# Search passes dealt to attention heads by summed engine loads in place of weights

## What is computed

```
dots  = relu(einsum('bqhd,bsd->bqhs', q_idx, k_idx))
score = einsum('bqh,bqhs->bqs', w_idx, dots)          # -inf where not visible
_, idx = top_k(score, 256)                            # ties to the lower index
out_b = softmax(q . k[idx] * 64**-0.5 - slope * |t - idx|) @ v[idx]
```

## Time and profile before

| | us |
|---|---|
| median of 3 runs (3246.18 to 3248.87) | 3247.67 |
| profiled execution | 3250.48 |
| its span | 3248.7 |
| TensorE busy (share of the span) | 2896.0 (89%) |
| VectorE busy | 1690.7 (52%) |
| ScalarE busy | 1570.1 (48%) |
| GpSimd busy | 320.7 (10%) |

### The profile page before, as it was taken

The page is one execution under the profiler, slowest core; times in us unless marked ns, Lnnn a source line. Parts: engine busy times, 40 slices in busy tenths (PEclk is TensorE's granted clock), DMA queues, the critical chain, the costliest instruction groups (busy, mean ns, idle before and its releaser), DMA issues. The chain is left out here.

```text
span 3248.7 us, 42237 instructions
## 1 busy us (share of the span) xinstructions
PE 2896.0 (89%) x14392; PEld 2341.5 (72%) x14392; DVE 1690.7 (52%) x3092; ACT 1570.1 (48%) x3006; POOL 320.7 (10%) x1001
## 2 busy tenths in 40 slices
PE   6578888787977897889898999999999999999998
PEld 3456566666766676678786888878888888888887
DVE  2246768686978868845454444244432544244433
ACT  0457787778787786884433222232223222232222
POOL 0112231212121120110011000000000000000000
PEclk8788988899988988899999999999999999999999
DMA  5000000000000001121456333343333433343333
GB/s 211 7 23 14 24 14 14 14 14 14 14 4 14 10 7 56 59 108 42 127 177 192 97 97 97 123 143 97 97 118 112 133 97 97 120 145 97 93 99 119
DMA packets 286884, 254.86 MB, mean 78 GB/s; under 512 B 8685, under 2 KB 238617, under 8 KB 286617
## 3 DMA queue, kind: packets, MB, share of 16 engines
q1 hardware_dynamic: 282584, 236.32, 23.4%
q10 hardware_dynamic: 4160, 16.78, 1.3%
HBM read 219.50 MB, written 33.57 MB: 78 GB/s over the span
## 5 line engine op out<-in xcount | busy, mean ns | idle before, releaser
L2045 ACT ACTIVATE p_hi<-raw 128x1024 fp32r<-128x1024 f32 x264 | 279.4, 1058 | 669.5 <-PE ubank L1979 339.1
L2124 DVE TENSOR_TENSOR p_lo<-raw,p_hi 128x1024 fp32r<-128x1024 f32 x264 | 323.4, 1225 | 405.1 <-ACT p_hi L2045 405.1
L1322 DVE TENSOR_SCALAR_CACHE_REDUCE above<-score,cand 128x384 uint8<-128x384 f32 (+6 forms) x224 | 315.8, 1410 | 4.4
L1172 ACT ACTIVATE signs<-score,pick 128x512 int8<-128x512 f32 (+6 forms) x224 | 304.4, 1359 | 27.7 <-POOL pick L684 19.2
L1150 ACT ACTIVATE logit<-tbank 128x512 f32<-128x512 f32 (+3 forms) x448 | 214.3, 487 | 210.7 <-PE tbank L903 207.8
L903 PE MATMUL tbank<-ident,logit 128*128 128x128 f32 x1336 | 252.4, 303 | 63.5 <-ACT logit L1140 56.0
L919 PE MATMUL obank<-vb,logit 128*128 128x64 f32 x2176 | 299.8, 283 | 0.0
L919 PEld LDWEIGHTS obank<-vb,logit 128*128 128x128 f32 x2176 | 293.7, 208 | 0.0
L1977 PE MATMUL gbank<-x_hi,p_hi 128*128 128x512 f32 x704 | 276.5, 393 | 14.8 <-DVE p_lo L2124 14.8
L788 PE MATMUL work<-w_in,h_T 128*128 128x512 f32 (+1 forms) x768 | 282.7, 515 | 0.7 <-ACT h_T L981 0.7
L1978 PE MATMUL gbank<-keys,p_hi 128*128 128x512 f32 x704 | 275.9, 392 | 0.0
(11 more groups left out here) (236 smaller groups left out, 5133.4 us busy)
## 6 DMA issues: line engine op xcount, KB each, us to landing
raw<-in_w_gate_up SPq DMA_DIRECT2D x176, 512.0 KB, 3.8
raw<-in_w_down SPq DMA_DIRECT2D x88, 512.0 KB, 3.8
w_in<-in_w_ada ACTq DMA_DIRECT2D x4, 4096.0 KB, 13.0
wada<-in_w_ada SPq DMA_DIRECT2D x4, 2048.0 KB, 15.6
row<-in_x SPq DMA_DIRECT2D x16, 512.0 KB, 3.9
mixT<-oT SPq DMA_DIRECT2D x32, 256.0 KB, 2.3
x_rows<-in_x SPq DMA_DIRECT2D x16, 512.0 KB, 4.6
x<-x_rows SPq DMA_DIRECT2D x16, 512.0 KB, 3.1
```

The costliest lines, as they stand in the source:

```text
L1172: nc.scalar.activation(signs[:, 0:L], score[:, b % 2, 0:L], ACT.Sign, scale=-1.0, bias=pick[:].bitcast(F32), accum_out=less_more[:]).then_ ...
L1322: link(nc.vector.tensor_scalar(above[:, 0:L], score[:, b % 2, 0:L], cand[:].bitcast(F32), None, ALU.is_ge, ALU.add, accum_out=count[:]), b ...
L2045: nc.scalar.activation(p_hi[:, s], raw[:, s], ACT.Copy).then_inc(panel_high, 1)
L2124: nc.vector.tensor_tensor(p_lo[:, s], raw[:, s], p_hi[:, s].bitcast(F32), ALU.subtract).then_inc(panel_ready, 1)
```

## The change

The weights and `spread` go. `loads` walks the list of steps without any search in it and adds up, for each slot, an estimate of what VectorE, ScalarE and TensorE do there, at rates written as constants; work that an engine does some heads later is put to the later slot. `deal_passes` first adds the closing steps. Then it goes 32 rounds; in each, every search places one pass in the slot of its window where the longest of the three sums grows least, with 0.15 of the engine's own sum and 0.1 for each pass already there added. A window begins at the slot behind which the scores are complete, as heads 0 to 3 of the A group. `all_steps` makes the list once with empty searches and once with the dealt ones; a step now carries its slot as well, so the two lists are its entries 5 and 6. The instructions themselves, the closing steps and every other step are as before.

```diff
...
-def vector_weight(b, slot):
...
-def scalar_weight(b, slot):
...
-def spread(weights, n):
...
 def search_slots(b):
...
         slots += [(it, "B", h) for h in range(HEADS)]
+    return slots
...
+COLUMN = 1.05
+FIXED = 0.06
+PASS_VECTOR = 0.39
+PASS_SCALAR = 0.50
+SIDE = {"vector": {"norm": 1.3, "gains": 0.9, "latent": 0.8, "latent_up": 1.2, "queries": 1.5},
+        "scalar": {"norm": 1.3, "transposes": 1.2, "latent": 2.8, "latent_up": 2.8, "queries": 3.0, "mod": 0.6},
+        "tensor": {"transposes": 1.0, "latent": 0.7, "latent_up": 2.2, "queries": 1.3, "mod": 4.0}}
+PROJ = {"vector": (0, 0, 0, 0, 0), "scalar": (0, 0.6, 0, 0.6, 2.2), "tensor": (3.5, 3.5, 3.5, 3.5, 2.8)}
+def streamed(cols):
+    return FIXED + COLUMN * cols / 1000
+def loads(steps, beside):
+    out = {"vector": {}, "scalar": {}, "tensor": {}}
+    slots, it = [], {}
+    for s in steps:
+        if s[0] == "head":
+            slots.append(s[4])
+    heads = [s[1:4] for s in steps if s[0] == "head"]
+    for engine in out:
+        out[engine] = {slot: 0.0 for slot in slots}
+    def put(engine, at, us):
+        if 0 <= at < len(slots):
+            out[engine][slots[at]] += us
+    i = -1
+    for s in steps:
+        if s[0] == "head":
+            i += 1
+            kind, b, h = s[1:4]
+            tiles = len(key_tiles(kind, b))
+            for _, n in key_chunks(kind, b):
+                put("vector", i, streamed(n) + 0.1)
+                put("tensor", i, 0.92 * n / 1000)
+                put("scalar", i + 2, streamed(n))
+            put("tensor", i + 2, 0.12 * tiles)
+            put("tensor", i + 3, 0.23 * tiles)
+            put("scalar", i + 1, streamed(P * tiles) + 0.35 + (0.3 if kind == "A" else 0))
+            if h == HEADS - 1:
+                put("vector", i + 4, 1.0)
+                put("tensor", i + 5, 0.5)
+                put("scalar", i + 6, 0.6)
+            continue
+        at = i if s in beside else i + 1
+        if s[0] == "scores":
+            n = key_chunks("B", s[1])[s[2]][1]
+            put("vector", at, IDX_HEADS * (streamed(n) + 0.1))
+            put("scalar", at, IDX_HEADS * streamed(n))
+            put("tensor", at, IDX_HEADS * 0.92 * n / 1000)
+            continue
+        for engine in out:
+            us = PROJ[engine][s[2]] if s[0] == "proj" else SIDE[engine].get(s[0], 0.0)
+            lag = LAG[engine].get(s[0], 0) if engine != "tensor" and s in beside else 0
+            put(engine, at + lag, us)
+    return out
+def deal_passes(load):
     vector, scalar = {}, {}
-    if searched_by_scalar(b):
-        wts = [scalar_weight(b, slot) for slot in slots[:-3]]
-        for slot, r in zip(slots, spread(wts, len(ON_SCALAR))):
-            scalar[slot] = [(b, ON_SCALAR[n]) for n in r]
-        for slot, action in zip(slots[-3:] + slots[-1:], AFTER_SCALAR):
+    searched = [b for b in range(NB) if P * (b + 1) > TOPK]
+    windows, counts = {}, {}
+    for b in searched:
+        slots = search_slots(b)
+        each = streamed(P * (b + 1))
+        scored = len(key_chunks("B", b))
+        if searched_by_scalar(b):
+            closing = zip(slots[-3:] + slots[-1:], AFTER_SCALAR)
+            windows[b] = slots[scored - 1:-3]
+        else:
+            closing = zip(slots[-2:] + slots[-1:], SEARCH[-3:])
+            windows[b] = slots[scored - 1:-2]
+        for slot, action in closing:
             vector.setdefault(slot, []).append((b, action))
-    else:
-        wts = [vector_weight(b, slot) for slot in slots[:-2]]
-        for slot, r in zip(slots, spread(wts, len(SEARCH) - 3)):
-            vector[slot] = [(b, SEARCH[n]) for n in r]
-        for slot, action in zip(slots[-2:] + slots[-1:], SEARCH[-3:]):
-            vector.setdefault(slot, []).append((b, action))
+            load["vector"][slot] += each * {"above": 1, "bias": 1}.get(action[0], 4 if action[1] == 0 else 2)
+        counts[b] = {slot: 0 for slot in windows[b]}
+    def longest(slot):
+        return max(load[engine][slot] for engine in load)
+    for _ in range(32):
+        for b in searched:
+            engine = "scalar" if searched_by_scalar(b) else "vector"
+            own = streamed(P * (b + 1)) + (PASS_SCALAR if engine == "scalar" else PASS_VECTOR)
+            def longer(slot):
+                more = load[engine][slot] + own
+                return max(more - longest(slot), 0.0) + 0.15 * more + 0.1 * counts[b][slot]
+            slot = min(windows[b], key=longer)
+            load[engine][slot] += own
+            counts[b][slot] += 1
+    for b in searched:
+        j = 0
+        into = scalar if searched_by_scalar(b) else vector
+        for slot in windows[b]:
+            for _ in range(counts[b][slot]):
+                into.setdefault(slot, []).insert(len(into.get(slot, [])), (b, ("bit", j)))
+                j += 1
+    for slot in vector:
+        vector[slot].sort(key=lambda x: x[0])
     return vector, scalar
...
-def mixing_steps():
+def mixing_steps(vector, scalar):
...
-    vector, scalar = {}, {}
-    for b in range(NB):
-        if P * (b + 1) > TOPK:
-            for all_of, mine in zip((vector, scalar), search_slots(b)):
-                for slot, actions in mine.items():
-                    all_of.setdefault(slot, []).extend(actions)
...
-            steps.append(("head", "A", nxt, h, tuple(vector.get(at, ())), tuple(scalar.get(at, ()))))
+            steps.append(("head", "A", nxt, h, at, tuple(vector.get(at, ())), tuple(scalar.get(at, ()))))
...
+@functools.cache
+def all_steps():
+    return mixing_steps(*deal_passes(loads(*mixing_steps({}, {}))))
```

More of the change, by code:

```diff
@@ L10 @@
+import functools
 from contextlib import ExitStack
@@ L318, in mixing_steps @@
         for h in range(HEADS):
-            steps.append(("head", "A", b, h, (), ()))
+            steps.append(("head", "A", b, h, (b - 2, "A", h), (), ()))
             front_a(b + 1, h)
@@ L339, in mixing_steps @@
             at = (b, "B", h)
-            steps.append(("head", "B", b, h, tuple(vector.get(at, ())), tuple(scalar.get(at, ()))))
+            steps.append(("head", "B", b, h, at, tuple(vector.get(at, ())), tuple(scalar.get(at, ()))))
             if b + 3 < NB:
@@ L357 @@
 SPLITS = {"latent": 2, "latent_up": 3, "queries": 2}
+@functools.cache
+def all_steps():
+    return mixing_steps(*deal_passes(loads(*mixing_steps({}, {}))))
 def engine_order(engine):
-    steps, beside = mixing_steps()
+    steps, beside = all_steps()
     out, late = [], []
@@ L404, in __init__ @@
     def __init__(self):
-        self.steps = mixing_steps()[0]
+        self.steps = all_steps()[0]
         self.heads = [s[1:4] for s in self.steps if s[0] == "head"]
@@ L725, in _ @@
                 if s[0] == "head":
-                    for b, action in s[5] + tuple(x for x in s[4] if x[1][0] == "above"):
+                    for b, action in s[6] + tuple(x for x in s[5] if x[1][0] == "above"):
                         move_pick(b, action)
@@ L1210, in _ @@
                 elif s[0] == "head":
-                    head(i, s[5])
+                    head(i, s[6])
                     i += 1
@@ L1475, in _ @@
                 elif s[0] == "head":
-                    head(i, *s[1:5])
+                    head(i, *s[1:4], s[5])
                     i += 1
@@ L1484, in raw_counts @@
     out, n = {}, 0
-    for s in mixing_steps()[0]:
+    for s in all_steps()[0]:
         n += s[0] in SPLITS
```

## The result

The changed kernel takes 3231.24 us (median of 5 runs, 3228.23 to 3234.43) against 3247.67: a ratio of 0.9947 [0.9936, 0.9957]. First the windows of the changed kernel, with the columns of the earlier trace rows: the heads; A.0-2, sum over blocks 6 to 14 (before: 165.30); A.3-7 of blocks 11, 12 and 14 with their sum; B.0-5 of block 8 with the sum; and the four stages of the end.

A forecast was written before the change was run, and what follows sets the result against it. The heads bound the kernel, with TensorE, VectorE and ScalarE at 71 to 83%, none full. Terms -35.3 - 7 + 15.7 - 4 + 3 - 2 + 2 + 4 sum to -23.6 us: forecast 3224, range 3192 to 3258.

The forecast's parts named there:

- (a): B heads 0-5, blocks 4 to 12: fewer vector and scalar passes, TensorE becomes longest, idle time unchanged: -35.3 us.
- (b): Head 0 of B blocks: fewer scalar passes stand before GpSimd's root, so it comes earlier: -7 us, ends 0 and -13.9.
- (c): A heads 3-7, blocks 6 to 14: added vector passes exceed free time, VectorE becomes longest: +15.7 us, ends 0 and +22.3.
- Rival (2): More gain: overflow of A heads 3-7 lands in the idle time at the root; 3201 us, chance 0.20.
- (3): Rival, no change: TensorE's granted clock falls to 0.85 in A heads 3-7; 3245 us, chance 0.12.
- Rival (1): Slower: VectorE holds the A heads and B heads give back little; 3269 us, chance 0.16.
- (d): A heads 0-2: VectorE, longest in the four odd blocks, loses 2 to 4 passes: -4 us, ends 0 and -10.
- (e): B heads 6-7, beside a search's ties: four more scalar passes: +3 us, 0 to +8, or +14 with GpSimd blocked.
- (f): Small blocks (A2 to A5, B0 to B3): about the same numbers of passes: -2 us, ends -5 and +3.
- (g): Count `above` in VectorE's head 5 after a scalar search: more passes just ahead in B2, B4, B6: +2 us.
- (h): The end: A15 heads 3-7 +13.0 us without slack, B13, B14 and A15 heads 0-2 shorter; together +4 us.

The follow-up runs named there:

- head1_free: Changed kernel, root where it was, without vector passes in head 1 of the B blocks (21 passes go elsewhere): 3215.77 us, 0.9889 of the kernel before.
- end_old: Changed kernel with the searches of blocks 14 and 15 back in their old places: 3228.87 us, 0.9936 of the kernel before.
- root_first: Changed kernel with GpSimd making the root for `gains` before it moves the thresholds of head 0: 3191.65 us, 0.9822 of the kernel before.
- rf_head1_free: Changed kernel with GpSimd's root ahead of head 0's threshold moves and no vector passes in head 1 of the B blocks: 3183.18 us, 0.9805.

## Why the prediction came out right, and where its steps were wrong

The forecast of 3224 was 7.2 us too low, its sign and range right. That it came so close is luck: (a) with (b) was off by 25 us and (c) by 17, in opposite directions, and the two errors cancelled for the greater part. B.0-5 came to 313.8 us, just under the 315 above which the prediction called (a) wrong.

**(a) and (b), -42.3 forecast, -17.1 measured in B.0-5.** Two errors. The first is a count: the sum took passes dealt to heads as passes that run in the window of those heads. The windows of VectorE's bit passes alone tell it: A.3-7 of block 12, the sum over blocks 6 to 14, and the sum of B.0-5 over blocks 4 to 12 (length, busy time, and instructions, two to a pass), before and after:

```profile
974.51:998.62 24.11, 11.11 (x11) 1.00 0.11 33
...
sum 213.74, DVE 93.75; mean DVE 10.42
...
sum 330.95, DVE 100.39; mean DVE 11.15
```

```profile
971.89:995.65 23.76, 15.61 (x16) 1.00 0.11 33
...
sum 212.00, DVE 117.14; mean DVE 13.02
...
sum 313.84, DVE 76.46; mean DVE 8.50
```

Block 12 was dealt 5 passes more, and 2.5 more run in the window. Over the nine blocks 44 passes were dealt to these heads before and 75 after, a difference of 31, but 59.5 ran in the windows before and 73 after: 13.5. In B.0-5 it is 15 fewer (62 to 47), not 25. Before the change, passes of neighbouring heads already ran within A.3-7. That fits the timeline: windows are cut at ScalarE's exponentials, and VectorE runs ahead of them (in the changed kernel it reads the first logits of B8 at 799.91, 1.1 us before the cut at 801.03); which pass belongs to which head was not read off one by one, but the passes dealt one head later (A heads 4 to 7 with head 0 of the B block behind, and B heads 1 to 6) number 58 and 67, and 59 and 47, close to what ran. ScalarE likewise: 56 passes to 40 in B.0-5, not 61 to 38, 26.7 us and not 36.7. With these counts ScalarE stays longest, at 251.6 us (measured 252.0), and (a) is -26.7. In blocks 9 to 12 that is what came: 21.2 us less of ScalarE's passes, and stages 19.6 shorter. In blocks 4 to 8 it is 5.5 less, and the stages got 2.5 longer.

The second error is the idle time, which (a) took as unchanged and (b) as shorter by 7. Nearly a third of B.0-5 is head 1, with the wait for the root ahead of it, and the change left it as it was: 99.8 us before, 98.1 after. The vector passes of head 1 run ahead of the logits that TensorE waits for. The text on the root named them as "what is late next" and put them "as now"; they were 12 in these nine blocks and are 13, but blocks 4 to 8 went from 6 to 9, and blocks 9 to 12 from 6 to 4. `head1_free` shows the price of all thirteen, 16.1 us of B.0-5, not of those that the deal added. In blocks 4 to 8 head 1 is 8.8 shorter there for nine passes, so the three added account for some 3 us (an estimate) of the 8.0 by which these blocks fall short of the count. The rest stays open.

**(b) alone.** The wait for the root was to fall to 52 and fell to 58.8. The root did come earlier: from the end of ScalarE's squares to its start, summed over B blocks 1 to 12, 63.0 us before and 48.5 after, 14.5 less (at most 13.9 forecast). VectorE, with no pass left in head 0 of B blocks 4 to 10, arrives earlier too, and its wait shrank by 6.3 only.

**(c), +15.7 forecast, -1.7 measured.** By the runs' count VectorE gains 23.4 us of passes, not 64.9, and 156.9 + 23.4 stays below TensorE's 206.1: in sum nothing overflows. Of the five stages that were to overflow only those of blocks 13 and 14 got longer, by 3.7 together. So the lower end held, though not for the reason given: with the root first, A.3-7 is 211.5, so it was not the idle time at the root that took the overflow. Rival (2) had (c) at the right size by a wrong mechanism. The clock of (3) did not fall: 1.00 in seven of the nine stages and 0.98 at least. Rival (1) priced (c) at +22.3, and its condition for B.0-5 came true (17.1 returned, under 38.8): it failed by A.3-7 alone.

**(d)** -4 forecast, -5.3 measured, but the four odd blocks that it argued from gave 2.0 of it, and 3.1 came in block 8, where the clock went from 0.91 to 1.00: the size was right in part by luck. **(e)** +3 forecast, +5.5 measured: 7.5 more in the odd blocks 5, 7, 9 and 11 (66.3 to 73.8), 2.1 less in the others. In those four a third scalar pass stands in head 6. Block 7 in the timeline:

```profile
744.18 2.55 DVE L1408 TENSOR_TENSOR_SCAN rank<-h_T 128x1152 f16<-128x1152 bf16 x1
...
748.18 1.42 DVE L1414 SCALAR_TENSOR_TENSOR h_T<-rank,need,h_T 128x1152 bf16<-128x1152 f16 x1
...
745.77 1.06 POOL L741 TENSOR_SCALAR pick_back<-less_more,toward 128x1 int32<-128x1 f32 x1 [1.74 <-ACT signs L1231]
748.76 1.00 POOL L741 TENSOR_SCALAR pick_back<-less_more,toward 128x1 int32<-128x1 f32 x1 [1.39 <-ACT signs L1231]
...
750.07 1.36 ACT L1231 ACTIVATE signs<-score,pick 128x1280 int8<-128x1280 f32 x1 [1.48 <-POOL pick L743]
```

GpSimd's step, 0.29 elsewhere, lasts until 0.1 to 0.2 us behind the end of VectorE's instruction, both times, and ScalarE's next pass waits 1.48 us. The rule quoted in the prediction from the Trainium skill ("SBUF — State Buffer", Who interferes with whom) agrees with the trace here: the scan takes its mask as both inputs, and the second instruction reads two arrays. The prediction's estimate of some 2 us per block lies near the 1.9 of the four (7.5 over 4), but that is no proof of it: the added passes alone take 6.2 us of ScalarE there, and the sum does not say how much the longer step adds. **(f) and (g):** the stages before A6 changed by -0.5 (forecast -2), the wait of `above` by +1.6 (forecast +2). **(h)** +4 forecast, +3.2 measured over all from A15 on; its parts came within 1.3 us each: A15.3-7 +14.0 for +13.0, B13.0-5 -4.7 and B14.0-4 -5.3 for -4 each, A15.0-2 -1.3 for -1. (Its lower end of -2 does not follow from its parts, which give -0.3; nothing hangs on it.)

## What to carry to other kernels

Before a planner of loads is improved, ask which in-order queue holds the wait: here the deal of 448 passes by loads won 0.5%, and moving a few small operations of GpSimd behind a root that others wait for won 1.1% alone and 1.3% more on top of it. A sum of loads per slot sees neither where in a slot a pass stands (ahead of the logits or behind: `head1_free`, which moves such passes, won 15.5 us) nor what is queued behind it. And when a trace is cut into stages, count the instructions that run in each window: engines run ahead of each other, and what is dealt to a head does not run within its window.

## What the runs showed that was not expected

A15.3-7 has TensorE at 42% of its time and a granted clock of 0.54 (0.73 before), and the end still costs only 3.2 us more: VectorE and ScalarE each fill 29 of its 32.6 us. That the clock costs little there `end_old` shows: the same stage took 18.67 us at 0.59, and 18.67 at 0.73 before. In B.0-5 of block 8 the clock counts: from `root_first` to `rf_head1_free` the stage gets 3.2 us shorter, and TensorE is busy 25.37 us in place of 28.90 for the same work, at 1.00 in place of 0.84. Its idle time is not less (3.40 and 3.78 us). In `root_first` the clock is at 0.50 (the 1.2 GHz level) from 783 to 788 us, behind a pause of 1.87 us, and at 0.51 from 806 to 808, behind one of 1.28; in `rf_head1_free` it is 1.00 (2.4 GHz) over the stage, though a pause of 1.54 us lies at its start. What lowers it these rows don't settle. Part of what such an edit gives goes with the clock, and no run separates it from the shorter wait.
